# A hybrid decoder step on one core: attention instructions reordered, window state copied DRAM to DRAM, sample values loaded during compression

## The reference, cut to what matters

```python
k_all = jnp.concatenate([kv_past[0], new_k], axis=1)      # past rows come by page_table
wk_all = jnp.concatenate([win_buf[0], k_w], axis=1)       # last 512 positions, per sample
o_win = window_sample(q, wk_all, wv_all, q_pos, pos0 - wbuf, slopes)
win_k, win_v = wk_all[:, -wbuf:], wv_all[:, -wbuf:]       # outputs too
kc = rms_norm(compress(k_all[:, :, 0], cmp_pe[0], cmp_w[0]), kc_gain)  # blocks of 32, stride 16
vc = compress(v_all[:, :, 0], cmp_pe[1], cmp_w[1])
o_cmp, p_cmp = gqa_attend(q, kc, vc, ...)                 # branch 1: compressed blocks
...                                                       # branch 2: top 16 blocks of 64 by p_cmp
o = gates[..., 0:1] * o_cmp + gates[..., 1:2] * o_slc + gates[..., 2:3] * o_win
```

## Time and profile before

| | |
|---|---|
| median of 3 runs | 2483.07 us (2475.38 to 2487.23) |
| the profiled execution: time, span | 2482.11 us, 2480.3 us |
| PE busy in the span | 2002.2 us (81%) |
| DVE, ACT, POOL busy | 850.2, 672.4, 732.2 us (34, 27, 30%) |
| compression, row loads of samples 1 to 7 | 230.25 to 356.27 us |
| end of compression | to 391.33 us |
| sample attention | 391.33 to 491.12 us |
| prompt attention | 491.1 to 700.9 us |

### The profile page before, as it was taken

The page is one execution under the profiler, slowest core; times in us unless marked ns, Lnnn a source line. Parts: engine busy times, 40 slices in busy tenths (PEclk is TensorE's granted clock), DMA queues, the critical chain, the costliest instruction groups (busy, mean ns, idle before and its releaser), DMA issues. The chain is left out here.

```text
span 2480.3 us, 46089 instructions
## 1 busy us (share of the span) xinstructions
PE 2002.2 (81%) x20699; PEld 1807.2 (73%) x20699; DVE 850.2 (34%) x1196; ACT 672.4 (27%) x972; POOL 732.2 (30%) x332
## 2 busy tenths in 40 slices
PE   6985775466678999997968886888666689999978
PEld 6974445344467999997948884888624679999968
DVE  2014332244423311312262214666298433113131
ACT  3221551144423312312222213222101233223121
POOL 2300000054442443432212221333262223443422
PEclk9986886577789999998978887999887799999989
DMA  4106763610011222222111100000210112222210
GB/s 163 52 1 212 224 194 119 211 46 1 1 52 68 86 105 92 86 103 68 52 52 68 52 20 11 4 4 4 78 49 9 68 52 98 99 86 103 86 52 35
DMA packets 93139, 183.73 MB, mean 74 GB/s; under 512 B 11615, under 2 KB 70887, under 8 KB 78991
## 3 DMA queue, kind: packets, MB, share of 16 engines
q1 hardware_dynamic: 92942, 180.79, 21.6%
HBM read 164.52 MB, written 16.25 MB: 73 GB/s over the span
## 5 line engine op out<-in xcount | busy, mean ns | idle before, releaser
L251 POOL TENSOR_TENSOR ws_t<-ring,ws_t 128x2048 fp32r<-128x2048 f32 x74 | 340.1, 4597 | 615.4 <-ACT ws_t L245 615.4
L228 PE MATMUL P<-uh,ws_t 128*128 128x260 f32 x2560 | 420.5, 286 | 35.0 <-DVE ul L264 35.0
L228 PEld LDWEIGHTS P<-uh,ws_t 128*128 128x128 f32 x2560 | 357.9, 191 | 37.7 <-issue 35.0
L228 PE MATMUL P<-hidh,ws_t 128*128 128x260 f32 x2176 | 350.9, 283 | 0.0
L228 PEld LDWEIGHTS P<-hidh,ws_t 128*128 128x128 f32 x2176 | 299.1, 188 | 0.0
L228 PE MATMUL P<-ul,ws_t 128*128 128x260 f32 x1280 | 260.9, 286 | 0.0
L1373 POOL TENSOR_SCALAR S_<-S_,st_ 128x128 f32<-128x128 f32 (+3 forms) x96 | 102.2, 1082 | 459.0 <-DVE st_ L1410 459.0
L245 ACT ACTIVATE ws_t<-ring 128x2048 fp32r<-128x2048 f32 x74 | 141.5, 1914 | 301.5 <-PE P L228 301.5
L228 PE MATMUL P<-hidl,ws_t 128*128 128x260 f32 x1088 | 218.9, 283 | 0.0
L228 PEld LDWEIGHTS P<-ul,ws_t 128*128 128x128 f32 x1280 | 200.1, 191 | 0.0
L228 PEld LDWEIGHTS P<-hidl,ws_t 128*128 128x128 f32 x1088 | 167.2, 188 | 0.0
(11 more groups left out here) (352 smaller groups left out, 3517.4 us busy)
## 6 DMA issues: line engine op xcount, KB each, us to landing
ring<-in_weights SPq DMA_DIRECT2D x104, 1024.0 KB, 4.7
ring<-in_rows SPq DMA_DIRECT2D x32, 384.0 KB, 4.5
raw<-in_rows SPq DMA_DIRECT2D x32, 384.0 KB, 4.7
vs<-in_cv_slc SPq DMA_DIRECT2D x64, 128.0 KB, 2.2
vw<-in_win_v SPq DMA_DIRECT2D x8, 512.0 KB, 4.3
out_win_v<-vw SPq DMA_DIRECT2D x8, 512.0 KB, 8.4
out_kv<-Z SPq DMA_DIRECT2D x1, 3120.0 KB, 10.8
xn<-in_win_k SPq DMA_DIRECT2D x12, 256.0 KB, 4.9
```

Of the source, the lines that this page charges most:

```text
L228: mm = pe.matmul(P[:, n // 2 % 2 * 4 + 2 * m + hf, 0:HT], w, xs[:, i * nk + k, hf * HT:(hf + 1) * HT], start=first_k and w is wh and xs is xh,
L251: pool.tensor_tensor(ws[:, u % 2, 1, :], ring[:, u % RING, :], ws[:, u % 2, 0, :].bitcast(F32), ALU.subtract).then_inc(wsplit_ready, 1)
```

## The change

There are five edits.

1. Compression no longer stores `win_k`, and the loads no longer wait for these stores. `win_v` is no longer stored in sample attention either. In their place prompt attention issues two DMAs from input to output in DRAM, of 4 MB each, behind its four weight loads.
2. One tensor `big` takes the place of `raw` and `XP` in compression, of `vs`, `vw` and `PT` in sample attention, and of `S_` and `PT_` in prompt attention.
3. So SP loads the five constants and the values of samples 0 to 2 while compression ends, and those of sample 3 once the sums of the prompt are done. The register read and the DMA alternate now.
4. In sample attention SP loads samples 4 and 6 and ACT loads 5 and 7, each after a `pv_done`. PE scores the prompt's compressed keys first, DVE adds their bias between two scalings, and PE turns them before sample 4.
5. In prompt attention PE's scores run three units ahead, and ACT alternates: two exponentials of unit u, one copy of unit u-2, two exponentials, one copy.

The core of the diff:

```diff
-                        for s in range(1, NS + 1):
-                            if s < NS:
-                                if s >= 2:
...
-                                    sp.wait_ge(stores, stored + 32 * (s - 1))
-                                load_rows(sp, s, raw[s % 2], kwin[s % 2])
-                            v = s - 1
-                            sp.wait_ge(rows_in[v % 2], 16 * (PAGES + 2) * (v // 2 + 1))
-                            for g in range(2):
-                                sp.dma_start(o["win_k"][v][:, g, :], kwin[v % 2][g]).then_inc(stores, 16)
+                        for s in range(1, NS):
+                            if s >= 2:
...
+                            load_rows(sp, s, raw[s % 2], kwin[s % 2])
+
+                        sp.wait_ge(scored, NS)
                         sp.wait_ge(cmp_done, 2 * NS)
                         sp.dma_start(to_rows, a["to_rows"]).then_inc(rows_const_in, 16)
                         sp.dma_start(from_rows, a["from_rows"]).then_inc(rows_const_in, 16)
+                        load_sample_constants(sp)
+                        for s in range(3):
+                            load_values(sp, s)
+                        sp.wait_ge(cmp_done, 2 * NS + 2)
+                        load_values(sp, 3)
                         sp.wait_ge(stores, state["stores"])
...
+                    def load_values(eng, s):
+                        for n in range(PAGES):
+                            page = eng.value_load(pages[0:1, s * PAGES + n:s * PAGES + n + 1], min_val=0,
+                                                  max_val=a["cv_slc"].shape[0] - 1)
+                            eng.dma_start(vs[:, s % VB, n, :], a["cv_slc"][bass.ds(page, 1)]
+                                          .rearrange("o p c -> (o p) c")).then_inc(v_in[s % VB], 16)
+                        eng.dma_start(vw[:, s % VB, :, :], a["win_v"][s]).then_inc(v_in[s % VB], 16)
...
+                        for s in (4, 6):
+                            sp.wait_ge(pv_done, s - VB + 1)
+                            load_values(sp, s)
...
-                            if s == 5:
+                            if s == 4:
                                 pe.wait_ge(cp_ready, 1)
...
+                        act.wait_ge(pv_done, 2)
+                        load_values(act, 5)
                         act.wait_ge(cmx_ready, 1)
                         act.activation(Pc, Pc, ACT.Exp).then_inc(cexp_done, 1)
                         act.wait_ge(cturned, 1)
...
+                        act.wait_ge(pv_done, 4)
+                        load_values(act, 7)
...
+                        for name in ("win_k", "win_v"):
+                            sp.dma_start(o[name].rearrange("s p a b -> (s p) (a b)"),
+                                         a[name].rearrange("s p a b -> (s p) (a b)")).then_inc(stores, 16)
...
-                            if u + 2 < NUN:
-                                scores(u + 2)
+                            if u + 3 < NUN:
+                                scores(u + 3)
...
-                                mm.then_inc(e_done, 1)
-                            if u >= 2:
...
-                                for g2 in range(2):
+                                    mm.then_inc(e_done, 1)
+                                if u >= 2:
```

More of the change, by code:

```diff
@@ L459, in layer0 @@
                     VCt = sb(c1, "VCt", [64, NS, 256])
-                    compress_and_score(xn, Z, KCb, VCt, VCp, KB, ring_rows, rows_in, load_rows)
+                    big = sb(c1, "big", [128, 6 * PAST + 2 * 2 * 2048])
+                    VB = 4
+                    vs = big[:, 0:8192].rearrange("p (s n c) -> p s n c", s=VB, n=PAGES)
+                    vw = big[:, 10240:14336].rearrange("p (s n c) -> p s n c", s=VB, n=WIN // 128)
+                    sbias = ring[:, 0, 0:NCOL]
+                    samegs = sb(c1, "samegs", [128, 128])
@@ L461, in layer0 @@
+                    compress_and_score(xn, Z, KCb, VCt, VCp, KB, ring_rows, big, rows_in, load_rows,
+                                       load_sample_constants, load_values)
                     PcT = sb(c1, "PcT", [128, NQ, 3, 128])
                     dist = sb(c1, "dist", [128, 512])
-                    sample_attention(xn, Z, gates, Vn, VCt, KCb, PcT, dist, pages)
-                    prompt_attention(xn, Z, gates, Vt, VCp, PcT, dist, KB)
+                    sample_attention(xn, Z, gates, Vn, VCt, KCb, PcT, dist, VB, vs, vw, big[:, 8192:8192 + 1920],
+                                     (sbias, samegs, blockno, own_sample, own_head), sample_in, v_in, load_values)
@@ L465, in layer0 @@
+                    prompt_attention(xn, Z, gates, Vt, VCp, PcT, dist, big, KB)
                 add_product(xn, list(range(U_OUT, U_OUT + 4)), "w_out")
@@ L1001, in build, with sample_attention @@
         gate_col = lambda gp, r, g2, b: 9 * (2 * gp + g2) + 3 * r + b
-        def sample_attention(mix, Z, gates, Vn, VCt, KCb, PcT, dist, pages):
+        def sample_attention(mix, Z, gates, Vn, VCt, KCb, PcT, dist, VB, vs, vw, pt, constants_, sample_in, v_in,
+                             load_values):
             with ExitStack() as ctx:
                 wide = ring[:, :, :].rearrange("p r c -> p (r c)")
-                S, bias = wide[:, 0:NCOL], wide[:, NCOL:2 * NCOL]
+                bias, samegs, blockno, own_sample, own_head = constants_
+                S = wide[:, UW:UW + NCOL]
                 Pc, cbias = (wide[:, c:c + NQ * HEADS * 32].rearrange("p (i h c) -> p i h c", i=NQ, h=HEADS)
-                             for c in (3584, 5632))
+                             for c in (2 * UW, 3 * UW))
                 cok = sb(ctx, "cok", [128, NQ, 1, 32])
@@ L1052, in sample_attention @@
                     + [(C_CMP, NC_S), (C_NSLC, NS), (C_NWIN, NS)]
[L1054 to L1068, removed]
                 with nc.Block(no_gpsimd_drain=True) as block:
@@ L1256, in _, with prompt_attention @@
                                              P[:, 1, 0:6 * NS].rearrange("p (s c) -> p s c", s=NS)))
-        def prompt_attention(mix, Z, gates, Vt, VCp, PcT, dist, KB):
+        def prompt_attention(mix, Z, gates, Vt, VCp, PcT, dist, big, KB):
             with ExitStack() as ctx:
                 SB = 4
-                S = sb(ctx, "S_", [128, SB, 4, 512])
-                PT = sb(ctx, "PT_", [128, 2, 4, 512])
+                S = big[:, 0:8192].rearrange("p (u j c) -> p u j c", u=SB, j=4)
+                PT = big[:, 8192:12288].rearrange("p (u j c) -> p u j c", u=2, j=4)
+                state["stores"] += 32
                 st = sb(ctx, "st_", [128, SB, 2, 4])
@@ L1327, in values @@
                             mm.then_inc(o_done, 1)
-                        scores(0)
-                        scores(1)
+                        for u in range(3):
+                            scores(u)
                         for u in range(NUN + 1):
-                            if u + 2 < NUN:
-                                scores(u + 2)
+                            if u + 3 < NUN:
+                                scores(u + 3)
                             if u < NUN:
```

122 lines of the change are left out of this document (54 added, 68 removed).

## The result

The changed kernel takes 2357.85 us (median of 4 runs, 2355.28 to 2362.31), the kernel before 2480.77 (4 runs, 2475.38 to 2487.23) on the same chip: a ratio of 0.9497, 95% interval 0.948 to 0.9514. The forecast was 2380 with a range of 2352 to 2422.

| stage | before | after | difference | forecast |
|---|---|---|---|---|
| up to the first row load | 230.25 | 232.00 | +1.8 | 0 |
| compression, first row load to last sum | 138.49 | 101.81 | -36.7 | -30 |
| end of compression | 22.59 | 41.26 | +18.7 | +16 |
| sample attention | 99.79 | 77.18 | -22.6 | -20 |
| prompt attention | 209.78 | 129.45 | -80.3 | -68 |

The account below looks back on a forecast made before the run. Bounds: a loop of waits in prompt attention, SP's list in compression, the values in sample attention. 2482 - 30 (compression) + 16 (its end) - 20 (sample attention) - 68 (prompt attention) = 2380 us, range 2352 to 2422.

Parts of the forecast that it names:

- rival (b): Prompt attention: with no waits left PE runs at its full clock, a period falls to some 19 us, kernel 2357; chance 0.13.
- I take PE's 13.3: Compression: the cycle falls from 18.3 us to PE's 13.3 of work on a sample, -30 us in all.
- the bound I gave for SP and the DMA engines, 12.3: Compression: SP's issuing and a sample's data at 299 GB/s each take 12.3 us a cycle, which would give -36.
- The price at SP's rate: Sample attention: ACT issues a sample's values at SP's 9.0 us, giving -20 us for the stage.
- small: Sample attention: the skill's view of issuing time; ACT's two loads would cost next to nothing, the sum about 2362.
- I take 22.8: Prompt attention: PE's work becomes the limit at 22.8 us a period, down from 34.10, giving -68 us.
- the 5.2 us beside them: Prompt attention: the 209.8 us stage less six periods of 34.10, kept unchanged in the forecast stage of 142 us.
- the 0.91 of the dense stretch: Granted clock in the output product behind prompt attention, taken as speaking for only part of the full-clock rival.
- The copies, forecast at nothing: Prompt attention: the two DRAM copies take 28 to 56 us within a stage of 142, costing nothing.
- Rival (a): Prompt attention: waits remain, POOL's 17.03 us and hand-overs in series, 28.5 us a period, kernel 2414; chance 0.21.
- (c): Gain given back: loads cost twice SP's price, compression gives 7 and prompt attention 34; 2491, no change; chance 0.05.
- (d): Slower: DRAM copies hold up the next weights in SP's queue; at 50 GB/s the kernel takes 2528; chance 0.04.

## Why the prediction was right, and where its terms were off

The sign and the cause of each stage's difference held; three terms of the sum were off in size. The measured 2357.85 lies in the range of 2352 to 2422 only because that reaches into rival (b); it is below the forecast's own band of 2360 to 2402. The profiled execution is 2362.31, 18 under the sum: 12.3, 6.7 and 2.6 us too little was given to prompt attention, compression and sample attention, 2.7 too little was charged for the end of compression, and the rest of the span grew by 1.2.

**Compression, -30 forecast, -36.7 measured.** The mechanism holds (the stores put back give 18.4 us a cycle). The step that failed is "I take PE's 13.3". The earlier trace rows show that work right after a wait of 4.08 us: its first scores took 3.13, and the same six products take 1.99 in the kernel after:

```profile
285.46 1.99 PE L889 MATMUL P<-ring,Z 128*64 128x512 f32 x6
```

Without the waits PE needs 12.2 us (60.78 / 5), and the cycle went to the bound I gave for SP and the DMA engines, 12.3, hence to the end of the range, -36. PE's 12.2 and that 12.3 lie too near each other to tell which of them binds now.

**End of compression, +16 forecast, +18.7 measured.** Right: 9.3 us a sample for 9.0. That register reads alternate with DMAs hides nothing, as I took from the row loads, and fixed pages show that they are the difference.

**Sample attention, -20 forecast, -22.6 measured.** The steps came in the forecast's order: samples 0 to 3 without a wait for their values, ScalarE's issuing 8.6 us ahead of its exponential, PE waiting 11.0 for the softmax and 5.3 for sample 7. The price at SP's rate, chosen against "small", held: ScalarE's 8.6 us a sample are close to SP's 9.0, and the run with SP alone shows that the split is worth its price. The 2.6 us lie in the last step, where sample 7's products were forecast at 71.1 us of the stage and began at 68.2 (443.26 - 375.07): ScalarE issued its loads in 8.2 us, beginning while the copy to `PcT` still ran.

**Prompt attention, -68 forecast, -80.3 measured.** Distance and order open the loop; both were tried apart. The step that failed is "I take 22.8", PE's work at the clock of 0.75. In the period the clock is 1.00 and PE needs 17.35, so rival (b), to which I gave 0.13, had the period (some 19) and its cause right. A second term failed the other way, "the 5.2 us beside them": after the change it is 16.5 (129.45 less six times 18.82). The 5.2 hid a quick start and a drain. DVE's first copy of a pair comes with the eighth of the 24 units, the fifth copy with the last unit. Before, the first eight units took 53.7 us (491.12 to 544.86), 14.5 less than two periods, and 18.3 more passed from the fifth copy to the last (681.52 to 699.84). After, the first eight take 36.3 (452.25 to 488.53), only 1.4 less than two periods, and the drain is 16.7 (563.83 to 580.55). With (b)'s period and 5.2 the stage would have taken 119, so that (b)'s time of 2357 came so near is luck: compression's 6.7 and sample attention's 2.6 made up most of these 10 us.

My argument against (b), the 0.91 of the dense stretch in the earlier trace rows, was no ceiling. What PE did before the clock moved is shown by slices of 2.5 us of the kernel before (same columns as the stretches):

```profile
644.80:647.30 2.50, 0.00 (x0) 0.00 (x0) 2.43 (x4) 0.34 (x1) 0.00 (x0) 0.81 0.00 0
647.30:649.80 2.50, 0.00 (x0) 0.00 (x0) 0.79 (x3) 2.50 (x9) 2.21 (x2) 0.50 0.00 0
649.80:652.30 2.50, 1.78 (x10) 1.48 (x12) 0.00 (x0) 1.17 (x4) 2.50 (x3) 0.50 0.00 0
...
657.30:659.80 2.50, 2.50 (x23) 1.80 (x22) 1.50 (x5) 0.81 (x1) 2.50 (x3) 1.00 0.00 0
```

and by slices of 5 us of the kernel after:

```profile
470.00:475.00 5.00, 5.00 (x28) 3.63 (x28) 3.35 (x9) 2.85 (x11) 5.00 (x5) 0.50 0.86 301
475.00:480.00 5.00, 5.00 (x50) 3.47 (x48) 3.15 (x9) 2.88 (x9) 5.00 (x6) 0.97 1.02 328
...
525.00:530.00 5.00, 3.78 (x36) 2.50 (x33) 4.02 (x16) 4.40 (x14) 3.65 (x3) 1.00 0.00 0
```

Before, two slices in which PE had nothing end at 1.2 GHz, and PE works on at 1.2 GHz for the next ones. After, PE is busy all through the slices from 470 and 475, the clock rises to 2.4 GHz, and it stays there up to 565, also in the slice from 525, in which PE is busy for 3.78 of 5.00 us. The Trainium skill (TensorE: Matmul & The Clock Gate, section HAM oscillation — how this bites in real kernels) says that after gaps the next group starts slow; the rows agree. In this loop a wait taken off PE paid twice, once as the wait and once as the clock (PE's 172 instructions of a period: 20.08 us at 0.85, 18.75 at 0.92, 17.35 at 1.00).

**The copies, forecast at nothing,** show no price in the run without them; the forecast of 28 to 56 us for them meets 34.1 to the last landing. Rival (a) needed 28.5 us a period; that is about what the distance of two leaves (28.4). Rivals (c) and (d) did not come.

## What to carry to other kernels

Busy time of TensorE that is read among waits holds the low clock in it: before it is used as the floor of a loop without waits, work it out at both levels of the granted clock. A hand-written distance between scores and their use has an optimum, here three, set by which engine must free the bank that the next scores need. What a loop's stage takes beside its periods changes with the loop: here the drain stayed (18.3 and 16.7 us) and the quick start went. Loads through a page table are to be priced on the issuing engine, with the register reads, and placed where no other engine waits behind them: moving them took another 28 us off the two stages (18.8 and 9.4).

## What I had not expected of the hardware

- The clock held 1.00 with PE 92% busy (17.35 of 18.82 us), above the 0.91 of the output product.
- Reading a page number before each DMA doubles the issuing: 9.3 us a sample with it, 4.3 to 5.7 without. Alternating reads and DMAs hides none of it.
- More work for PE (+0.76 us a period) or less for POOL (-3.8) moved a loop in which both are over 90% busy by +0.06 and -0.39 us.
